# First loads on two queues, the first projection half by half, and a divided last scaling, in a three-block float32 kernel

## What is computed

```python
def _rms_f32(xf, g):
    return xf * lax.rsqrt(jnp.mean(xf * xf, axis=-1, keepdims=True) + EPS) * g.astype(jnp.float32)

def hybrid_mixer(h, w_in, w_gate2, b_gate, g_gla, g_q, g_k, w_out):
    proj = h @ w_in
    cuts = np.cumsum([GLA_DK, GLA_DK, GLA_DV, GLA_DV, GLA_GATE_RANK, SB_D, SB_D])
    gq, gk, gv, gr, glr, sq, sk, sv = jnp.split(proj, cuts, axis=-1)
...
    h = x
...
    return rmsnorm(h, norm_final)
```

## Time and profile before

| what | value |
|---|---|
| median of three runs | 1216.69 us |
| the profiled execution's own time | 1215.55 us |
| its span | 1213.7 us |
| busy: TensorE, VectorE, ACT, POOL | 1190.9, 913.8, 673.0, 177.8 us |
| chain that ended last | TensorE 94% of the span, VectorE 2%, ACT 1%, POOL 1% |
| DMA, mean | 182 GB/s |

### The profile page before, as it was taken

How to read it: one execution, slowest core, us unless ns; L and a number is a source line. 1 busy time by engine, 2 the same in 40 slices (tenths; PEclk the granted TensorE clock), 3 DMA queues, 4 the chain that set the end, 5 groups by cost and what they waited for, 6 DMA issues and landing times.

```text
span 1213.7 us, 14269 instructions
## 1 busy us (share of the span) xinstructions
PE 1190.9 (98%) x5534; PEld 977.7 (81%) x5534; DVE 913.8 (75%) x1126; ACT 673.0 (55%) x811; POOL 177.8 (15%) x171
## 2 busy tenths in 40 slices
PE   7998999999999999999999999999999999999997
PEld 6776888888887888888888888888888888888886
DVE  6676788878668888887788887646477656888884
ACT  6664565556545565564565564554434444766552
POOL 1400032220200032220032220000000000322200
PEclk9999999999998999999999999999999999999999
DMA  9432465555441455554455554655453454555540
GB/s 332 174 139 70 160 232 205 208 208 213 167 158 68 175 208 208 208 185 167 168 208 208 207 187 166 267 204 178 184 194 139 142 204 141 208 188 192 182 182 35
DMA packets 32470, 220.71 MB, mean 182 GB/s; under 512 B 3745, under 2 KB 4145, under 8 KB 6674
## 3 DMA queue, kind: packets, MB, share of 16 engines
q1 hardware_dynamic: 32402, 219.79, 50.0%
HBM read 218.72 MB, written 1.05 MB: 181 GB/s over the span
## 4 chain that ended last, share of the span: by engine, by line
PE 94%; DVE 2%; ACT 1%; POOL 1%; issue 1%; DMA 0%; SPq 0%; POOLq 0%; DVEq 0%; ACTq 0%
PE ps L258 29%; PE ps L260 29%; PE ps L259 29%; PE ps L266 4%; PE ps L263 4%; POOL st L389 1%; DVE wlo L217 1%; ACT whi L210 1%; POOL AR L886 0%; ACT AR L365 0%; ACT xh L356 0%; DMA kc<-in_cst 0%; DVE state L1129 0%; ACT AR L1039 0%; DVE st L1160 0%
## 5 line engine op out<-in xcount | busy, mean ns | idle before, releaser
L217 DVE SCALAR_TENSOR_TENSOR wlo<-raw,whi 128x2048 fp32r<-128x2048 f32 x166 | 382.2, 2306 | 126.3 <-ACT whi L210 96.1
L258 PE MATMUL ps<-whi,xh 128*128 128x512 f32 x1116 | 440.8, 395 | 0.4 <-DVE xl L421 0.4
L260 PE MATMUL ps<-whi,xl 128*128 128x512 f32 x1116 | 435.0, 390 | 0.0
L259 PE MATMUL ps<-wlo,xh 128*128 128x512 f32 x1116 | 434.9, 390 | 0.0
L210 ACT CAST whi<-raw 128x2048 fp32r<-128x2048 f32 x163 | 311.8, 1913 | 182.8 <-PE ps L260 181.4
L258 PEld LDWEIGHTS ps<-whi,xh 128*128 128x128 f32 x1116 | 209.5, 188 | 50.3 <-issue 1.8
L260 PEld LDWEIGHTS ps<-whi,xl 128*128 128x128 f32 x1116 | 209.5, 188 | 45.0
L259 PEld LDWEIGHTS ps<-wlo,xh 128*128 128x128 f32 x1116 | 209.7, 188 | 41.1
L258 PE MATMUL ps<-whi,yh 128*128 128x512 f32 x348 | 139.7, 401 | 1.6 <-DVE yl L1071 1.6
L260 PE MATMUL ps<-whi,yl 128*128 128x512 f32 x348 | 136.1, 391 | 0.0
L259 PE MATMUL ps<-wlo,yh 128*128 128x512 f32 x348 | 135.6, 390 | 0.0
(11 more groups left out here) (234 smaller groups left out, 1191.1 us busy)
## 6 DMA issues: line engine op xcount, KB each, us to landing
raw<-in_w SPq DMA_DIRECT2D x199, 1024.0 KB, 4.8
raw<-in_w SPq DMA_DIRECT2D x4, 256.0 KB, 4.2
raw<-in_w SPq DMA_DIRECT2D x2, 512.0 KB, 6.7
AR<-in_b_pw SPq DMA_DIRECT2D x1, 1024.0 KB, 4.7
AR<-in_gate_bias SPq DMA_DIRECT2D x1, 1024.0 KB, 8.4
AR<-in_dft SPq DMA_DIRECT2D x1, 864.0 KB, 8.7
AR<-in_rmask SPq DMA_DIRECT2D x1, 768.0 KB, 10.0
AR<-in_pmat SPq DMA_DIRECT2D x1, 768.0 KB, 11.2
```

What stands on the lines that cost most here:

```text
L217: e.scalar_tensor_tensor(out=wlo[:, v % S, :], in0=raw[:, v % R, :], scalar=1.0, in1=whi[:, v % S, :].bitcast(F32), op0=ALU.mult, op1=ALU. ...
L258: e.matmul(o, ah, bh, start=start, stop=False, skip_group_check=skip)
L259: e.matmul(o, ah, bl, start=False, stop=False, skip_group_check=skip)
L260: return e.matmul(o, al, bh, start=False, stop=stop, skip_group_check=skip)
```

## The change

Four things change, in the opening and at the end.

**Loads.** SP issues the left half of x of row block 0, the four pieces of unit 0, the left half of row block 1, and unit 1. ACT issues the identity, the parameters (before its table load) and the two right halves of x (after it).

**First projection.** TensorE multiplies unit 0 with both row blocks and then unit 1 with both. Within a quarter the four high-high products come first, then the four high-low, then the four low-high. Three products on a tile of zeros, which nothing reads, are put in: two at the start and one behind the first transposes.

**ACT and VectorE in the opening.** The first piece of unit 0 is cast before the first half of x; the halves follow in the new order; and unit 2's cast (and low part) stands ahead of row block 1's square (and variance).

**The end.** For row block 0, VectorE multiplies with the final weights before the root is there, and ACT scales. For row block 1, VectorE scales 640 columns and ACT 384, and ACT stores its own part on its own queue.

```diff
-                return sig.at("x0%d" % half if t == 0 else "x1", 0)
+                return sig.at(f"x{t}{half}", 0)
...
+        def tensor_warm(e, n):
+            for _ in range(n):
+                mm(e, ps[5][:, 0:256], sts[0][:, 0, 0:P], sts[0][:, 0, :])
+
+        def tensor_high(e, q, t, j):
+            q.wait_ge(*sig.at("xh", "mix0", t, j))
+            for k in range(4):
+                q.wait_ge(*sig.at("hi_piece", j, k if j == 0 else k // 2))
+                mm(e, ps[4 + t][:, :], xh[:, 4 * j + k, tcols(t)], whi[:, j, 512 * k:512 * k + 512], j == 0 and k == 0, False)
+
+        def tensor_high_low(e, q, t, j):
+            for k in range(4):
+                q.wait_ge(*sig.at("lo_piece", j, k if j == 0 else k // 2))
+                mm(e, ps[4 + t][:, :], xh[:, 4 * j + k, tcols(t)], wlo[:, j, 512 * k:512 * k + 512], False, False)
+
+        def tensor_low_high(e, q, t, j):
+            q.wait_ge(*banks.emptied("x", "mix0", t, j))
...
         def tensor_hybrid(e, q):
             x = x_of("mix0")
+            q.wait_ge(*sig.at("zeros", 0))
+            tensor_warm(e, 2)
             q.wait_ge(*sig.at("ld_ident", 0))
             turn_x(e, q, "mix0", None, 0, 0)
...
+            tensor_warm(e, 1)
...
+            tensor_high(e, q, 0, 0)
+            tensor_high_low(e, q, 0, 0)
+            tensor_low_high(e, q, 0, 0)
+            turn_x(e, q, "mix0", None, 1, 0)
             turn_x(e, q, "mix0", None, 0, 1)
...
+            tensor_high(e, q, 1, 0)
+            tensor_high_low(e, q, 1, 0)
+            tensor_low_high(e, q, 1, 0).then_inc(*sig.up("used", 0))
             turn_x(e, q, "mix0", None, 1, 1)
-            quarter(e, q, "sq", u, 0, 1, 4, xh, xl, x)
-            quarter(e, q, "sq", u, 1, 0, 5, xh, xl, x)
-            quarter(e, q, "sq", u, 1, 1, 5, xh, xl, x)
+            tensor_high(e, q, 0, 1)
...
+            tensor_low_high(e, q, 1, 1).then_inc(*banks.full("sq", 1))
+            sig.alias("used", (1,), "full5", ("sq", 1))
...
         def scalar_hybrid(e, q):
+            e.dma_start(ident, cst[:, 0:P]).then_inc(*sig.up("ld_ident", 0, by=16))
+            e.dma_start(pr[:, :], par).then_inc(*sig.up("ld_par", 0, by=16))
             e.preload_act_table_set("natural_log_exp_and_others")
+            for t in range(2):
+                e.dma_start(h[:, t, 512:1024], xin[t][:, 512:1024]).then_inc(*sig.up(f"x{t}1", 0, by=16))
+            hi_piece(e, q, 0, 4, 0)
             q.wait_ge(*sig.at("ld_par", 0))
             norm_half_act(e, q, "mix0", 0, 0)
-            for k in range(4):
+            for k in range(1, 4):
                 hi_piece(e, q, 0, 4, k)
+            norm_half_act(e, q, "mix0", 1, 0)
             norm_half_act(e, q, "mix0", 0, 1)
             hi_piece(e, q, 1, 2, 0)
             hi_piece(e, q, 1, 2, 1)
-            norm_half_act(e, q, "mix0", 1, 0)
             norm_half_act(e, q, "mix0", 1, 1)
             norm_square(e, q, "mix0", None, 0)
+            hi(e, q, 2)
             norm_square(e, q, "mix0", None, 1)
-            hi(e, q, 2)
             hi(e, q, 3)
...
+        LEFT = 640
...
         def scalar_out(e, q):
             norm_square(e, q, "out", "n2", 0)
+            q.wait_ge(*sig.at("rstd", "out", 0))
+            q.wait_ge(*sig.at("gained_first", 0))
+            e.activation(res[:, 0, :], res[:, 0, :], ACT.Copy, bias=0.0, scale=rstd[:, 0:1]).then_inc(*sig.up("out", 0))
...
-            e.activation(res[:, 1, 512:1024], res[:, 1, 512:1024], ACT.Copy, bias=0.0,
+            e.activation(res[:, 1, LEFT:D], res[:, 1, LEFT:D], ACT.Copy, bias=0.0,
                          scale=rstd[:, 1:2]).then_inc(*sig.up("out_right", 1))
+            q.wait_ge(*sig.at("out_right", 1))
+            e.dma_start(out[1][:, LEFT:D], res[:, 1, LEFT:D]).then_inc(*sig.up("stored_right", 1, by=16))
...
         def vector_out(e, q):
+            q.wait_ge(*sig.at("ld_fin", 0))
+            for half in range(2):
+                q.wait_ge(*h_at("n2", 0, half))
+            e.tensor_tensor(res[:, 0, :], h[:, 0, :], fin, ALU.mult).then_inc(*sig.up("gained_first", 0))
             norm_var(e, q, "out", 0)
-            q.wait_ge(*sig.at("rstd", "out", 0))
-            q.wait_ge(*sig.at("ld_fin", 0))
-            e.scalar_tensor_tensor(out=res[:, 0, :], in0=h[:, 0, :], scalar=rstd[:, 0:1], in1=fin, op0=ALU.mult,
-                                   op1=ALU.mult).then_inc(*sig.up("out", 0))
...
-            q.wait_ge(*sig.at("gained", 1, 0))
-            e.tensor_scalar(res[:, 1, 0:512], res[:, 1, 0:512], rstd[:, 1:2], None, ALU.mult).then_inc(*sig.up("out_left", 1))
+            q.wait_ge(*sig.at("gained", 1, 1))
+            e.tensor_scalar(res[:, 1, 0:LEFT], res[:, 1, 0:LEFT], rstd[:, 1:2], None, ALU.mult).then_inc(*sig.up("out_left", 1))
...
             load(h[:, 0, 0:512], xin[0][:, 0:512], "x00")
-            load(pr[:, :], par, "ld_par")
-            load(ident, cst[:, 0:P], "ld_ident")
...
                 if v == 0:
-                    load(h[:, 0, 512:1024], xin[0][:, 512:1024], "x01")
-            load(h[:, 1, :], xin[1], "x1")
+                    load(h[:, 1, 0:512], xin[1][:, 0:512], "x10")
...
-            for half in range(2):
-                cols = slice(512 * half, 512 * half + 512)
-                q.wait_ge(*sig.at(("out_left", "out_right")[half], 1))
-                e.dma_start(out[1][:, cols], res[:, 1, cols]).then_inc(*sig.up("stored", 1, half, by=16))
-            q.wait_ge(*sig.at("stored", 1, 1))
+            q.wait_ge(*sig.at("out_left", 1))
+            e.dma_start(out[1][:, 0:LEFT], res[:, 1, 0:LEFT]).then_inc(*sig.up("stored", 1, by=16))
+            q.wait_ge(*sig.at("stored", 1))
+            q.wait_ge(*sig.at("stored_right", 1))
```

More of the change, by code:

```diff
@@ new lines, in tensor_high_low @@
+        def tensor_high_low(e, q, t, j):
[4 more added lines that the diff above has]
+            q.wait_ge(*banks.emptied("x", "mix0", t, j))
+            for k in range(4):
+                last = mm(e, ps[4 + t][:, :], xl[:, 4 * j + k, tcols(t)], whi[:, j, 512 * k:512 * k + 512], False,
+                          j == 1 and k == 3)
+            return last
@@ L1181, in tensor_hybrid @@
-            turn_x(e, q, "mix0", None, 0, 1)
-            q.wait_ge(*x(0, 0))
-            for k in range(4):
-                q.wait_ge(*sig.at("lo_piece", 0, k))
-                mm(e, ps[4][:, :], xh[:, k, 0:P], wlo[:, 0, 512 * k:512 * k + 512], False, False)
-                mm(e, ps[4][:, :], xl[:, k, 0:P], whi[:, 0, 512 * k:512 * k + 512], False, False)
-            turn_x(e, q, "mix0", None, 1, 0)
-            turn_x(e, q, "mix0", None, 1, 1)
-            quarter(e, q, "sq", u, 0, 1, 4, xh, xl, x)
@@ new lines, in tensor_hybrid @@
+            tensor_high_low(e, q, 1, 0)
+            tensor_low_high(e, q, 1, 0).then_inc(*sig.up("used", 0))
+            turn_x(e, q, "mix0", None, 1, 1)
+            tensor_high(e, q, 0, 1)
+            tensor_high_low(e, q, 0, 1)
+            tensor_low_high(e, q, 0, 1).then_inc(*banks.full("sq", 0))
+            tensor_high(e, q, 1, 1)
+            tensor_high_low(e, q, 1, 1)
+            tensor_low_high(e, q, 1, 1).then_inc(*banks.full("sq", 1))
+            sig.alias("used", (1,), "full5", ("sq", 1))
@@ L1349, in vector_hybrid @@
         def vector_hybrid(e, q):
+            lo_piece(e, q, 0, 4, 0)
             q.wait_ge(*sig.at("ld_par", 0))
             norm_half_dve(e, q, "mix0", 0, 0)
-            for k in range(4):
+            for k in range(1, 4):
                 lo_piece(e, q, 0, 4, k)
+            norm_half_dve(e, q, "mix0", 1, 0)
             norm_half_dve(e, q, "mix0", 0, 1)
```

11 lines of the change are left out of this document (3 added, 8 removed).

## The result

The changed kernel has a median of 1219.70 us over six runs (1217.77 to 1220.97), against 1215.99 of the kernel before on the same chip: a ratio of **1.0031, 95% interval 1.0021 to 1.0042**. That is 3.7 us slower, just over the 3.65 us that I had called telling from no change, and 0.1 us above my range. The profiled execution took 1219.66 us around a span of 1217.8; before, 1215.55 around 1213.7.

What follows compares the result with a forecast made beforehand. TensorE bounds 94% of the span, so an edit pays only at the two ends. POOL's chain +0.75 and the end -0.45 sum to +0.3 us, 1217.0 on the median's scale; 8-in-10 range 1213.6 to 1219.6.

Steps and rivals of the forecast that it cites:

- sign of being wrong: Opening: the forecast is wrong if TensorE starts the second projection over 1 us from 22.8 us.
- The landing (8.75): Opening loads: unit 0's fourth piece lands at 8.75 us, a middle between 7.9 and 9.6; its low part ends at 10.1.
- my upper end of 9.6: Opening loads: the fourth piece's landing if x's right halves (512 KB, 1.7 us) pass ahead of unit 0's last pieces.
- Rival (a): Opening loads: x's right halves pass unit 0's pieces, which land at 9.6; +1.15 us in all, 1217.8; chance 0.20.
- my 7.9: Opening loads: the fourth piece's landing by issue times alone, with two issues fewer ahead of it on SP.
- The first quarter (five products at 0.23): First projection on TensorE: after the low part at 10.1, five products at 0.23 us end at 11.25, four transposes at 11.7.
- Rival (b): First projection: TensorE stays at 1.2 GHz through the second quarter because it pauses twice; 3.8 us more, 1220.8; chance 0.07.
- The wait of the second projection (22.8): Opening: unit 2's low part ends at 22.65, so TensorE starts the second projection at 22.8 instead of 23.00.
- POOL's chain (+0.75): Opening: unit 3's low part ends at 25.8, not 25.05, so POOL's chain of powers and multiplies, and TensorE, start 0.75 us later.
- TensorE waits for POOL twice: Expected in the new profile: TensorE waits for POOL near 32 and 39 us.
- The products on zeros (nothing): Opening: three added products, at most 0.76 us each, cost nothing unless the identity lands late; they may raise the clock.
- The end (-0.45): Kernel's end: right residual half added at 1207.15, not 1207.62; both stores start together near 1210.25; 0.45 us less in all.

Runs made afterwards that it cites:

- the new end alone: The kernel before with only the changed end, its opening kept; median 1214.52 us against 1215.77, ratio 0.9991.
- the scaling earlier on ACT: The changed kernel, but ACT scales row block 0's "sq" right behind unit 2's cast, ahead of the second square and unit 3's cast; median 1219.16 us, ratio 1.0033.
- the squares alone: The changed kernel with ACT's two squares moved behind unit 0's last cast, its loads kept; median 1215.41 us, ratio 1.0004 to the kernel before.
- the old order: The changed kernel with the opening programs of TensorE, ACT and VectorE of before, without products on zeros; median 1216.36 us, ratio 1.0010 to the kernel before.
- both squares earlier: The changed kernel with x's right halves issued by SP and ACT's two squares behind unit 0's last cast; median 1214.16 us, ratio 0.9996 to the kernel before.

## Why the prediction was wrong

I forecast +0.3 us and it was +3.7. The direction I gave the least chance, 0.08, is the one that came, by a hair beyond the 0.3%. The working fails in three terms of the opening and has no term for a fourth cost, the clock's fall; the end is rightly described. My own sign of being wrong came: the second projection started 4.4 us from 22.8.

**The landing (8.75).** The fourth piece landed at 10.3, beyond even my upper end of 9.6, and its low part was done at 11.70, not at 10.1: +1.6. I put the right halves "at about 3 us", behind the table load. The trace shows the two issues at 1.70 to 2.60, so they went out beside SP's second and third pieces and ahead of the fourth, and not behind them. Rival (a) named the mechanism and understated its size: without the halves the piece landed at 7.8, as my 7.9 has it, and with them 2.5 us later in that pair of profiles, not 1.7. The Trainium skill (DMA: Bandwidth & Descriptors, section "Issuing engines are not separate DMA queues") says that DMAs of several issuing engines interleave on the same 16 DMA engines. The trace agrees: the third piece and the second right half, issued 0.03 us apart on two queues, landed within about 0.2 us of each other, 9.6 and 9.8. Nothing was overtaken; the halves were simply issued ahead of the fourth piece.

**The first quarter (five products at 0.23).** The sum had the upper level from 10.1 us on, and no row gave it: before, it came at 12.2. From that low part to the transposes I had 1.15 us; it took 2.64 (11.70 to 14.34), since the level rose only at 13.3: +1.5. Rival (b) had this mechanism with a price of 3.8, and I tied it to the second quarter, which did run at 0.23. Its condition (0.42 apart at 15 us) was not met, its first part was paid. My argument that the new kernel "has done more by 12.9" compared sums of work; in fact TensorE waited 2.00 us for the third piece just ahead of 10.26. How much of the 1.5 is due to the change is open: with the opening of before unchanged (the new end alone) the level also came at about 13.3 and not at 12.2.

From the transposes to unit 2's cast the working holds: 7.25 forecast, 7.39 measured.

**The wait of the second projection (22.8).** This is the step that failed in kind. I let TensorE start when unit 2's low part was done. But ACT's line 867 must also have emptied bank 4, and it stands behind both squares and the casts of units 2 and 3. By my own schedule unit 3's cast ended at 23.5, so line 867 could end at 24.2 at the earliest and TensorE not start at 22.8: the forecast contradicted itself. Measured: from unit 2's cast to the start 5.44 us instead of 4.3, +1.1. In the kernel before the same release had stood just ahead of 23.00, with no idle time beside it to show it; in the new end alone it is a wait of 0.17 us. The order of ACT's program, shown ahead of the prediction, ends one line short of it. Two experiments show it by moving line 867 earlier: the scaling earlier on ACT, and the squares alone.

The three are 1.6 + 1.5 + 1.1, with 0.1 between: 22.8 becomes 27.1.

**The clock behind the wait.** None of my cases had it. The 2.05 us wait was followed by 3.5 us at half clock, 1.6 us. One experiment fills the wait, the squares alone remove it, and in both profiles the clock stays up.

**POOL's chain (+0.75).** This term of the sum was not the path: TensorE came so late that the heads were ready at both places. That takes 0.66 off +4.17 and +1.6; another 0.42 of them is not resolved. My "TensorE waits for POOL twice" was wrong here, and right where the scaling stood earlier.

**The products on zeros (nothing).** Right for the time, with a wrong price: one took 1.03 us, not at most 0.76. The first two ended at 3.4, ahead of the identity (transposes from 4.03), so they cost nothing; nor did they bring anything clear, as the kernels without them and with more of them show.

**The end (-0.45).** The mechanism is right to the hundredth up to the scaling: VectorE adds the right half at 1211.60, 0.04 behind TensorE's end at 1211.56, and the scaling starts 0.46 us earlier against that end. The stores are what I expected too, no gain: the part behind the scaling went from 3.65 to 3.77. In all -0.34.

**Range and chances.** The case I took for the likeliest left out three costs of the same sign, and each had been within sight: an issue time, a clock level, a release. The range ended at 1219.6, and the median came at 1219.70.

## What to carry to other kernels

Before costing a moved step, list all that each waiting instruction of the bound engine waits for, a PSUM bank's last reader too, and follow the engine that gives each signal one instruction further than seems needed: here a release without idle time before became the longest wait after. When work is grouped by weights and not by tokens, look for what falls out of the other engines' idle time; the squares belonged in the 4 us in which ACT now waited, and moving them brought the time level with before. A load on another queue is not free while the first pieces are on their way: here the first loads landed in the order of issue over both queues, ahead of the pieces issued behind them.

## What the runs showed of the hardware

**A wait can cost twice.** In the changed kernel, with the right halves on SP's queue, and without products on zeros, waits of 2.02 to 2.06 us ahead of the second projection were each followed, at once or 0.8 to 1.6 us later, by a stretch with products 0.43 us apart. Behind the 1.00 us wait (the scaling earlier) and the 0.19 (the old order) the clock stayed up. The same happens elsewhere in these kernels, in some executions and not in others. The kernel before, a window behind waits of 0.75 and 1.60 us:

```profile
385.00:390.00 5.00, 4.59 (x14) 3.38 (x13) 4.40 (x11) 4.54 (x12) 0.93 (x1) 0.50 0.00 0
```

The kernel with both squares earlier near 105 us, where TensorE had waited 3.43 us for VectorE's line 1044:

```profile
105.00:110.00 5.00, 4.29 (x16) 3.26 (x17) 4.83 (x11) 0.11 (x1) 0.00 (x0) 0.66 0.00 0
```

That wait is as long in the kernels before and after, whose column reads 1.00 there. So the fall is no fixed consequence of the wait; what else decides it stays open. A fall lasted about 3.5 us (26.9 to 30.6 in the changed kernel) or about 6.8 us (384.5 to 391.3 in the kernel before), and a busy TensorE loses half of that, 1.7 or 3.4 us. Of the thirteen profiled executions eleven had one between 104 and 118 us and ten one between 384 and 400. The times within one kernel go with it: 27 executions of the kernel before took 1213.40 to 1213.67 us at a mean granted clock of 0.998, 1214.46 to 1216.34 at 0.996, and 1215.61 to 1216.81 at 0.993. Which falls make up each is not shown, as only one execution of each kernel has a trace.

**The clock column can be blind in the opening.** In twelve of the thirteen profiles it reads 1.00 up to 20 us, while products are 0.43 us apart until 8 to 16 us; only their spacing tells. In the thirteenth, with more products on zeros, the level had risen at 4 us and fallen again, and there the column shows it: 0.75 in 5 to 10 us and 0.56 in 10 to 15. The upper level that lasted came between about 8 and 16 us in openings that differ little.

**DMA issues run beside a table load.** ACT's two issues ran at 1.70 to 2.60 us while its table load ran from 1.67 to 2.95.

**Two queues stored no faster than one.** 320 KB and 192 KB issued 0.07 us apart landed in 2.5 and 2.6 us; before, two of 256 KB behind each other on one queue in a median of 2.2.
